# A 31-tap depthwise convolution moved to four-tap products: five of eight channel tiles on TensorE, its layer norm in two token halves

## The reference, cut to what matters

```python
def conformer_conv(h, pw1_w, pw1_b, dw_w, dw_b, ln_g, ln_b, pw2_w, pw2_b):
    a = h @ pw1_w + pw1_b
    u, g = jnp.split(a, 2, axis=-1)
    u = u * jax.nn.sigmoid(g)
    u = lax.conv_general_dilated(u, dw_w[:, None, :], window_strides=(1,),
        padding=[(15, 15)], dimension_numbers=("NWC", "WIO", "NWC"),
        feature_group_count=D_MODEL) + dw_b
    mu = jnp.mean(u, axis=-1, keepdims=True)
    var = jnp.mean(jnp.square(u - mu), axis=-1, keepdims=True)
    u = (u - mu) * lax.rsqrt(var + NORM_EPS) * ln_g + ln_b
    return jax.nn.silu(u) @ pw2_w + pw2_b
```

## Time and profile before

| what | value |
|---|---|
| median of 3 runs | 2560.32 us |
| lowest, highest | 2557.99, 2567.19 us |
| the profiled execution's own time | 2553.68 us |
| its span | 2551.5 us |
| TensorE busy | 2474.1 us, 97% |
| VectorE, ScalarE, GpSimd busy | 1333.3, 1154.1, 23.7 us |
| mean granted TensorE clock | 0.993 |

### The profile page before, as it was taken

How to read it: one execution, slowest core, us unless ns; L and a number is a source line. 1 busy time by engine, 2 the same in 40 slices (tenths; PEclk the granted TensorE clock), 3 DMA queues, 4 the chain that set the end, 5 groups by cost and what they waited for, 6 DMA issues and landing times.

```text
span 2551.5 us, 40614 instructions
## 1 busy us (share of the span) xinstructions
PE 2474.1 (97%) x16133; PEld 2118.5 (83%) x16133; DVE 1333.3 (52%) x2003; ACT 1154.1 (45%) x1827; POOL 23.7 (1%) x37
## 2 busy tenths in 40 slices
PE   7999999999999999999999999999989999979998
PEld 5777788886777778777788876999869999968998
DVE  4323333896633233433233367655777666786665
ACT  4333223465433332333332248654566655666654
POOL 0000000000000000000000000000100000100000
PEclk9999999999999999999999999999999999999999
DMA  8444452210344442244432230455414554513554
GB/s 327 165 164 167 186 186 86 99 50 1 116 164 166 178 166 99 105 174 165 164 132 99 99 116 26 173 197 197 183 71 178 191 205 167 203 51 116 197 195 151
DMA packets 52727, 374.93 MB, mean 147 GB/s; under 512 B 5822, under 2 KB 7034, under 8 KB 8736
## 3 DMA queue, kind: packets, MB, share of 16 engines
q1 hardware_dynamic: 50000, 358.63, 38.0%
q0 software_dynamic: 2208, 14.37, 1.6%
q10 hardware_dynamic: 432, 0.73, 0.1%
HBM read 372.55 MB, written 7.39 MB: 149 GB/s over the span
## 4 chain that ended last, share of the span: by engine, by line
PE 88%; DVE 7%; ACT 2%; issue 1%; DMA 1%; SPq 0%; ACTq 0%; DVEq 0%
PE acc L1908 27%; PE acc L1909 26%; PE acc L1910 26%; PE bank L1991 2%; DVE wlo L1355 1%; DVE prod L638 1%; PE bank L2018 1%; DMA ada_raw<-in_slabs 1%; DVE split_x L1440 1%; DVE sc L1809 1%; PE acc L2397 1%; ACT sc L1244 1%; DVE prod L1726 1%; PE acc L2423 0%; PE Mod L2001 0%
## 5 line engine op out<-in xcount | busy, mean ns | idle before, releaser
L1355 DVE TENSOR_TENSOR wlo<-raw,whi 128x1024 fp32r<-128x1024 f32 x534 | 645.7, 1223 | 868.8 <-ACT whi L814 867.8
L814 ACT ACTIVATE whi<-raw 128x1024 fp32r<-128x1024 f32 x534 | 556.4, 1056 | 929.8 <-PE acc L1910 868.1
L1908 PE MATMUL acc<-split_x,whi 128*128 128x256 f32 (+1 forms) x2808 | 935.4, 333 | 13.3 <-DVE split_x L1440 9.4
L1910 PE MATMUL acc<-split_x,wlo 128*128 128x256 f32 (+1 forms) x2808 | 920.5, 328 | 0.0
L1909 PE MATMUL acc<-split_x,whi 128*128 128x256 f32 (+1 forms) x2808 | 920.5, 328 | 0.0
L1908 PEld LDWEIGHTS acc<-split_x,whi 128*128 128x128 f32 x2808 | 527.7, 188 | 100.4 <-issue 36.5
L1910 PEld LDWEIGHTS acc<-split_x,wlo 128*128 128x128 f32 x2808 | 527.9, 188 | 50.0
L1909 PEld LDWEIGHTS acc<-split_x,whi 128*128 128x128 f32 x2808 | 528.3, 188 | 48.7 <-issue 1.7
L1908 PE MATMUL acc<-split_g,whi 128*128 128x512 f32 (+1 forms) x1056 | 351.3, 333 | 0.0
L1910 PE MATMUL acc<-split_g,wlo 128*128 128x512 f32 (+1 forms) x1056 | 351.1, 333 | 0.0
L1909 PE MATMUL acc<-split_g,whi 128*128 128x512 f32 (+1 forms) x1056 | 351.1, 332 | 0.0
(11 more groups left out here) (299 smaller groups left out, 2272.2 us busy)
## 6 DMA issues: line engine op xcount, KB each, us to landing
raw<-in_slabs SPq DMA_DIRECT2D x329, 1024.0 KB, 4.8
ada_raw<-in_slabs SPq DMA_DIRECT2D x10, 1024.0 KB, 25.6
skew_dram<-lines_dram POOLq DMA_DIRECT2D x1, 6144.0 KB, 24.1
bt<-skew_dram POOLq DMA_DIRECT2D x4, 1024.0 KB, 9.4
x<-in_x_in SPq DMA_DIRECT2D x1, 2048.0 KB, 18.0
mlp<-in_slabs POOLq DMA_DIRECT2D x2, 1024.0 KB, 6.1
out<-x SPq DMA_DIRECT2D x1, 1024.0 KB, 4.8
rope<-in_rope POOLq DMA_DIRECT2D x1, 512.0 KB, 3.7
```

Of the source, the lines that this page charges most:

```text
L814: nc.scalar.activation(whi[:, n % 2, cols], raw_of(n, cols), ACT.Copy).then_inc(ready, 1)
L1355: nc.vector.tensor_tensor(wlo[:, n % 2, cols], raw_of(n, cols), whi[:, n % 2, cols].bitcast(F32), ALU.subtract).then_inc(low, 1)
L1908: nc.tensor.matmul(out, w[0], xx[0], start=first, stop=False)
L1910: return nc.tensor.matmul(out, w[1], xx[0], start=False, stop=last)
```

## The change

Tiles 3 to 7 go to TensorE, tiles 0 to 2 stay with VectorE. TensorE no longer multiplies with diagonals of one tap. The partitions of a matmul operand are now 32 channels times 4 shifts: `u4[32 k' + c]` holds channel c shifted by k' tokens, and `diag` has at row 32 k' + c and column c the tap 4q + k' of that channel. One plain fp32 matmul (K = 128, 32 output partitions, 512 tokens) thus adds four taps of 32 channels; 8 of them (q, `QUADS`) make the 31 taps (the 32nd is set to zero) and 4 channel groups make a tile: 32 matmuls a tile, 160 in all, each channel group going to its own 32 partitions of a PSUM bank. Banks `B[1]` and `B[3]` take turns.

The shifted copies are made by DMA: GpSimd's queue stores each of the tiles 3 to 7 of `ubuf` in DRAM and loads it four times with the shifts. VectorE makes the operand `diag` of a tile in one multiplication. ScalarE's 186 instructions for diagonals and all splitting of taps and of `u` are gone, and so are the first `stay_busy` and the wait `x_final` ahead of the convolution.

The sum for the mean is now made by VectorE for seven tiles (6 additions, `total`) and finished by two matmuls instead of eight. Subtraction (now reading the sum in PSUM), squares, sum of squares, root and reciprocal run for tokens 0 to 255 and then 256 to 511; the squares go to `ubuf`, one place each, so that none waits for a buffer. The last `stay_busy` has 24 matmuls instead of 32.

```diff
-DVE_EARLY, DVE_LATE, PE_TILES = (0, 1), (2, 3, 4), (5, 6, 7)
-EARLY, CHAIN = 2 * (CONV_W - 1), 5 * (CONV_W - 1)
+DVE_EARLY, DVE_LATE, PE_TILES = (0, 1), (2,), (3, 4, 5, 6, 7)
+EARLY, CHAIN = 2 * (CONV_W - 1), 3 * (CONV_W - 1)
+GROUP = 32
+SHIFTS = P // GROUP
+QUADS = -(-CONV_W // SHIFTS)
+RING = 4
...
         def conv_out(j):
-            return acc[:, e // 2, e % 2, :]
+            return B[1 + 2 * ((j - PE_TILES[0]) % 2)][:, :]
...
+            def shifted_tiles(st, i):
+                mine = [j for j in (2 * i, 2 * i + 1) if j in PE_TILES]
+                if mine:
+                    pool.wait_ge(acc_free[(st.m0 + 1) % 2], freed(st.m0 + 1) + i)
+                for j in mine:
+                    e = j - PE_TILES[0]
+                    pool.dma_start(u_d[e], ubuf[:, j, :, :].rearrange("p s t -> p (s t)")).then_inc(u_stored[e], 16)
+                for j in mine:
+                    e = j - PE_TILES[0]
+                    pool.wait_ge(u_stored[e], 16)
+                    if e >= RING:
+                        pool.wait_ge(tile_done, e - RING + 1)
+                    for k in range(SHIFTS):
+                        src = bass.AP(u_d.tensor, e * P * 2 * SP_ + k,
+                                      [[2 * SP_, GROUP], [2 * SP_ * GROUP, SHIFTS], [1, SHIFTED]])
+                        pool.dma_start(u4[GROUP * k:GROUP * k + GROUP, e % RING, :, 0:SHIFTED], src)\
+                            .then_inc(u4_landed[e], 16)
...
             def conv(st):    # ScalarE
-                u_high(6)
-                u_high(7)
-                for b in range(2, BLOCKS):
-                    diagonals(b)
...
+                for e, j in enumerate(PE_TILES):
+                    act.wait_ge(tile_done, e + 1)
+                    b = VCOL["dw_b"] + j
+                    nc.scalar.activation(v[:, j, :], conv_out(j), ACT.Identity, bias=vec[:, b:b + 1])\
+                        .then_inc(conv_read, 1)
                 preload(ACT.Sqrt)
...
+                for s in range(2):
+                    for c in range(DT):
+                        if (s, c) == (1, 2):
+                            ln_root(0)
+                        cols = slice(S * s, S * s + S)
+                        act.wait_ge(d_ready, DT * s + c + 1)
+                        nc.scalar.activation(ln_sq[:, c, cols], v[:, c, cols], ACT.Square).then_inc(sq_ready, 1)
+                ln_root(1)
...
+            def total(j, first=None):
+                if j in PE_TILES:
+                    dve.wait_ge(conv_read, j - PE_TILES[0] + 1)
...
+                nc.vector.tensor_tensor(prod[:, 0, :], v[:, j, :], other, ALU.add).then_inc(added, 1)
...
+            def diagonals(e):
+                dve.wait_ge(w4_ready, SHIFTS - CONV_W % SHIFTS)
+                if e >= 2:
+                    dve.wait_ge(tile_done, e - 1)
+                taps = w4[:, :, e, 0:SHIFTS * (QUADS - 1) + 1:SHIFTS]
+                nc.vector.tensor_tensor(diag[:, e % 2, :, :, :], across(across(groups[:, :], QUADS), SHIFTS),
+                                        across(taps, GROUP, 3), ALU.mult).then_inc(diag_ready, 1)
...
             def conv(st):    # VectorE
-                u_low(6)
-                u_low(7)
-                chain(69, CHAIN)
+                for e in range(1, len(PE_TILES)):
+                    diagonals(e)
+                    chain(EARLY + 7 * e - 7, EARLY + 7 * e)
+                    if e > 1:
+                        total(PE_TILES[e - 2])
+                    else:
+                        total(DVE_EARLY[1], DVE_EARLY[0])
+                chain(EARLY + 28, CHAIN)
+                total(PE_TILES[3])
+                total(DVE_LATE[0])
                 dve.wait_ge(mean_done, 1)
-                step.done(nc.vector.tensor_scalar(rs[:, :], B[2][:, :], 1.0 / D, None, ALU.mult))
-                for c in range(DT):
-                    nc.vector.tensor_tensor(v[:, c, :], v[:, c, :], rs[:, :], ALU.subtract).then_inc(d_ready, 1)
-                dve.wait_ge(std_ready, st.std0 + 1)
-                step.done(nc.vector.reciprocal(rs[:, :], rs[:, :]))
+                for s in range(2):
+                    cols = slice(S * s, S * s + S)
+                    for c in range(DT):
+                        nc.vector.scalar_tensor_tensor(v[:, c, cols], B[2][:, cols], -1.0 / D, v[:, c, cols],
+                                                       ALU.mult, ALU.add).then_inc(d_ready, 1)
+                for s in range(2):
+                    cols = slice(S * s, S * s + S)
+                    dve.wait_ge(std_ready, st.std0 + s + 1)
+                    ins = nc.vector.reciprocal(rs[:, cols], rs[:, cols])
...
             def conv(st):    # TensorE
-                stay_busy(13)
-                x_final(pe, st)
...
+                for e, j in enumerate(PE_TILES):
+                    pe.wait_ge(u4_landed[e], 16 * SHIFTS)
+                    pe.wait_ge(diag_ready, e + 1)
+                    if e >= 2:
+                        pe.wait_ge(conv_read, e - 1)
+                    for q in range(QUADS):
+                        for k in range(SHIFTS):
+                            moving = u4[:, e % RING, k, :].rearrange("p (s t) -> p s t", s=2)[:, :, SHIFTS * q:SHIFTS * q + S]
+                            ins = nc.tensor.matmul(conv_out(j)[GROUP * k:GROUP * k + GROUP, :], diag[:, e % 2, k, q, :], moving,
+                                                   start=(q == 0), stop=(q == QUADS - 1))
+                    ins.then_inc(tile_done, 1)
+                pe.wait_ge(added, DT - 2)
+                nc.tensor.matmul(B[2][:, :], ones, prod[:, 0, :], start=True, stop=False)
+                pe.wait_ge(conv_read, len(PE_TILES))
+                nc.tensor.matmul(B[2][:, :], ones, v[:, PE_TILES[-1], :], start=False, stop=True).then_inc(mean_done, 1)
+                for s in range(2):
...
-                stay_busy(32)
+                stay_busy(24, B[2])
```

More of the change, by code:

```diff
@@ L235, in plan_with_counts @@
         at["n"] += st.slabs
-        groups = dict(up=22, pw1=8, down=4, pw2=4, wo=4, plegate=4, pleproj=2, conv=2)
+        groups = dict(up=22, pw1=8, down=4, pw2=4, wo=4, plegate=4, pleproj=2)
         at["m"] += st.slabs if st.kind in ("qkv", "qknorm", "nsa", "att") else groups.get(st.kind, 0)
@@ L276, in plan_with_counts @@
             st.summed |= st.carried
-            at["sq"] += 0 if st.summed else DT
-            at["sum"] += 1 if st.summed else DT
-            at["std"] += 1
+            at["sq"] += 0 if st.summed else DT if st.kind == "norm" else 2 * DT
+            at["sum"] += 1 if st.summed else DT if st.kind == "norm" else 2
+            at["std"] += 1 if st.kind == "norm" else 2
         if st.kind not in ("mods", "pleload", "pleproj"):
@@ L765, in _ @@
                     pool.dma_start(skew_d, bass.AP(lines_d.tensor, 0, [[0, P], [1, NH * 768]])).then_inc(skew_done, 16)
+                if st.kind == "pw1":
+                    pool.wait_ge(slab_used, st.n0 + 1)
+                    shifted_taps()
+                    for i in range(4):
+                        shifted_tiles(st, i)
                 if st.kind == "qkv":
@@ L2178, in mean_of @@
-                def mean_of(c, first=False, last=False):
-                    return nc.tensor.matmul(B[2][:, :], ones, v[:, c, :], start=first, stop=last)
-                m = st.m0 + 2
-                pe.wait_ge(conv_dve, CHAIN)
-                for j in DVE_EARLY + DVE_LATE:
-                    mean_of(j, first=(j == 0))
-                pe.wait_ge(acc_free[0], 1 + (m + 1) // 2)
-                pe.wait_ge(acc_free[1], 1 + m // 2)
-                for j in PE_TILES:
-                    ins = mean_of(j, last=(j == PE_TILES[-1]))
@@ new lines, in conv @@
+                pe.wait_ge(added, DT - 2)
[3 more added lines that the diff above has]
+                for s in range(2):
+                    cols = slice(S * s, S * s + S)
+                    for c in range(DT):
+                        pe.wait_ge(sq_ready, st.sq0 + DT * s + c + 1)
+                        ins = nc.tensor.matmul(B[1 + 2 * s][:, cols], ones, ln_sq[:, c, cols],
+                                               start=(c == 0), stop=(c == DT - 1))
+                    ins.then_inc(sum_done, 1)
```

139 lines of the change are left out of this document (52 added, 87 removed).

## The result

| | before | after |
|---|---|---|
| first comparison, median (lowest to highest) | 2562.73 us (2557.99 to 2567.19), 4 runs | 2514.48 us (2510.69 to 2521.95), 4 runs |
| ratio, 95% interval | | 0.9833, 0.9815 to 0.9850 |
| second comparison, median | 2559.47 us (2555.25 to 2566.7), 15 runs | 2522.97 us (2516.56 to 2526.55), 5 runs |
| ratio, 95% interval | | 0.9849, 0.9829 to 0.9868 |
| profiled execution: own time, span | 2553.68, 2551.5 us | 2521.95, 2520.1 us |

What follows compares the result with a forecast made beforehand. TensorE, busy 97% of the span, was taken as the bound. Convolution and mean -35.8, layer norm -5.0 and clock +1.0 gave -39.8 us: forecast 2519 us, own range 2510 to 2526, 8-in-10 range 2508 to 2532.

Steps and rivals of the forecast that it cites:

- TensorE's tiles at 6.9 us: Convolution on TensorE: 64 records a tile, four column groups beside each other, 6.9 us a tile, 34.5 us for five.
- simple scaling (8.0): Convolution on TensorE: a tile costed as eight times the 1.00 us slab of the modulation, 8.0 us; not taken.
- rival 1: Convolution: column groups overlap only by a factor of 3, 9.2 us a tile, 2527 us in all; chance 0.16.
- rival 2: Convolution: lower clock throughout with 32-column matmuls, tiles of 13.8 us, gain 6 us, 2554 us; chance 0.06.
- Rival 3, no overlap: Convolution: the four groups' products run one behind the other, 27.5 us a tile, 2619 us; chance 0.05.
- The rounds of VectorE: Convolution: diag, seven chain instructions at 0.785 us and an addition make 7.4 us a round, just over TensorE's 6.9.
- VectorE last by some 2 us: End of the convolution: VectorE finishes at 569.3, some 2 us after TensorE's last tile at 567.0.
- The copies at nothing: Shifted copies through DRAM for tiles 6 and 7: landed by 548, needed at 552.7, cost nothing, cover 0 to 5 us.
- The layer norm, -5.0: Layer norm in two halves: second reciprocal ends 10.7 us after the mean instead of 15.7, -5.0 us.
- The clock, +1.0: Layer norm: pauses on TensorE lower the clock and lengthen the sums of squares, +1.0 us (bounds 0 and 2.5).
- -35.8: Convolution and mean: VectorE begins to subtract at 571.2 instead of 606.99, -35.8 us.

Runs made afterwards that it cites:

- late copies: Changed kernel with ten dependent GpSimd multiplications put ahead of the loads of the shifted copies of tiles 6 and 7; first subtraction 4.1 us later.

## Why the prediction was right

- *TensorE's tiles at 6.9 us.* 34.93 / 5 = 6.99 us, with VectorE's diagonals holding the blocks a little; without that 34.55 / 5 = 6.91. The step from a slab of 256 tokens to a tile of 512 by the count of records, with one fill for all, was right; simple scaling (8.0) was not. So rival 1 (blocks of 9 us) is out, and rival 2 too, as the clock is 1.00 in the convolution. The five tiles were evacuated at 538.70, 545.49, 552.35, 559.34 and 566.47, which is 6.79, 6.86, 6.99 and 7.13 us apart, so the last two blocks waited 0.1 and 0.3 us for VectorE's diagonal, as forecast in kind. The rule of the Trainium skill's page "TensorE: Matmul & The Clock Gate", Part 3, that weight loads pass running matmuls only in another row group, is not what these runs show for column groups: 320 loads, busy for 11.17 us, lie within 34.85 us of running matmuls. Its 2.38 for three column tiles is below what this kernel reached with four: 27.5 / 6.9 = 4.0, where the 27.5 is the prediction's estimate of serial work, 64 records at 0.43 us.
- *Rival 3, no overlap*, was wrong for this order and partly real for another: the order of the loops decides, which the prediction did not see. It thought of the length of a matmul as the risk. That the changed kernel issues the groups in turns was luck, as far as the prediction goes.
- *The rounds of VectorE.* 0.785 us per dependent chain instruction was right (5.48 for seven: six steps of 0.79 and one whole). The round took 7.13 us (537.77 to 544.90) instead of 7.4, because an addition costs 0.60, a diag 1.14 and the last of the seven chain instructions 0.66 when the next instruction does not depend on it. This is the main part of the 1.06 us by which the subtraction came earlier than 571.2.
- *VectorE last by some 2 us.* 1.71 us of idle time on TensorE, ended by the addition, and 1.9 us gained when VectorE is relieved.
- *The copies at nothing.* Right: tile 6 landed near 550.1 (548 forecast) and was needed at 552.2, 2.2 us to spare within the 0 to 5 given. The margin was thinner than the forecast's 4.7.
- *The layer norm, -5.0.* Measured -4.96; 580.85 - 570.14 = 10.71 us against 10.7. But its cause is double: 3.75 us from the new norm itself and 1.2 us from the clock, which the prediction treated as a cost to come and not as one to go. The subtractions were 0.33 us apart (5.39 for sixteen), not 0.40; TensorE's sums set the pace, so this earned nothing.
- *The clock, +1.0.* This term failed. No pause of the changed kernel in the convolution or its norm is followed by the lower clock, in either of its traces. With it left out, the sum -35.8 - 5.0 = -40.8 is 1.0 us from the measured -41.8.

What stays open: why the clock falls in the kernel before, in both of its traces at the same place, and not with the same norm and the same pause of 2.17 us behind the new convolution. Length of the pause alone does not explain it, and the late copies show the lower clock in the convolution, behind pauses of 2.22 and 1.96 us. Open too is the pace of the late stages.

## What to carry to other kernels

Plain fp32 products of 512 tokens with 32 output partitions ran four at a time here only where the order of issue brought other column groups within about four records. Put the loop over groups innermost, or keep runs of one group to at most two such products. When a product leaves the bounding engine, write the schedule of both engines tile by tile: here the gain of 30 us on TensorE was matched to 2 us by VectorE's rounds, and a few instructions moved ahead gave those back. Judge a part of a few microseconds by its place in the profile, relative to a mark before the edit, as totals of this kernel scatter by 10 us.

## What the runs showed of the hardware

- The reach of TensorE over column groups: 16 records of one group in a row 20.7 us a tile, 8 records 14.0, 4 records and 2 records 6.9 to 7.0, against an estimated 27.5 for serial work. All of it is for fp32 products over 512 tokens.
- VectorE slows while GpSimd computes: seven chain instructions over 512 elements took 7.21 us instead of 5.48 beside GpSimd's multiplications, in the one trace of the one kernel that had them.
- The granted clock: at the lower level (0.50) in 611 to 613 us in both traces of the kernel before, at the upper one in the layer norm of all other traces, one of them with an equally long pause of 2.17 us. It cost 1.2 us there. With late copies it was 0.50 in 558 to 560, in the convolution, and cost 1.7 us.
- A load of 285 KB from DRAM, the fourth of tile 6, landed 10.7 us after issue in the changed kernel and 6.6 us after issue with late copies, where it was issued 10.5 us later.
- Late stages of equal code ran at 0.113 or about 0.118 us a matmul of 256 columns, at full clock, and the slower pace was at 1980 to 2010 us in one trace of the changed kernel and at 1610 to 1640 in the other.
